# Two spare words ahead of the activations h and hh, and two behind them

## The reference, cut to what matters

```python
def modulate(x, g, shift, scale):
    return rms_norm(x, g) * (1.0 + scale[:, None, :]) + shift[:, None, :]

def swiglu(h, w_gate, w_up, w_down):
    return (jax.nn.silu(h @ w_gate) * (h @ w_up)) @ w_down

# first block, twice: x + 0.5 g * swiglu(h ...); x + g * mixer(h); x + 0.5 g * swiglu(h ...)
# second block, twice: proj = h @ w_in -> mixer -> x;  q = h2 @ peer_q, expert sums over h2 -> x
```

## The kernel before

| tensor | start | past a multiple of 64 |
|---|---|---|
| ring | 16512 | 0 |
| weights_hi | 32896 | 0 |
| arena | 49280 | 0 |
| more_lo | 80000 | 0 |
| x | 180352 | 0 |
| h (h_lo) | 188544 | 0 |
| hh (h_hi) | 196736 | 0 |
| vfirst | 204928 | 0 |
| work; work_1 (gat_lo) | 215072; 219168 | 32 |
| small (gat_hi) | 223264 | 32 |

## Time and profile before

### The profile page before, as it was taken

How to read it: one execution, slowest core, us unless ns; L and a number is a source line. 1 busy time by engine, 2 the same in 40 slices (tenths; PEclk the granted TensorE clock), 3 DMA queues, 4 the chain that set the end, 5 groups by cost and what they waited for, 6 DMA issues and landing times.

```text
span 3476.7 us, 68787 instructions
## 1 busy us (share of the span) xinstructions
PE 3342.0 (96%) x26804; PEld 3203.1 (92%) x26804; DVE 2579.5 (74%) x4576; ACT 1608.5 (46%) x2594; POOL 198.7 (6%) x331
## 2 busy tenths in 40 slices
PE   6999989999999998999999999999899999999998
PEld 5999869999967998889999999998789999999998
DVE  7889667888736896746977867776755977777776
ACT  3456644454445445134444444444414445444444
POOL 1100001101000220200000000000300000000000
PEclk9999999999999999999999999999999999999999
DMA  9964218979613993034664466665215665456665
GB/s 369 359 221 169 74 49 324 336 261 334 249 46 113 385 374 127 31 132 171 228 207 169 166 225 229 230 229 174 75 46 171 230 221 175 169 203 229 232 228 181
DMA packets 246578, 707.46 MB, mean 203 GB/s; under 512 B 27472, under 2 KB 93008, under 8 KB 244928
## 3 DMA queue, kind: packets, MB, share of 16 engines
q1 hardware_dynamic: 212112, 571.64, 47.2%
q0 software_dynamic: 34224, 132.46, 10.2%
HBM read 669.40 MB, written 34.60 MB: 202 GB/s over the span
## 4 chain that ended last, share of the span: by engine, by line
PE 85%; DVE 7%; DMA 4%; ACT 2%; issue 2%; SPq 0%; POOL 0%; DVEq 0%; ACTq 0%; POOLq 0%
PE psum L517 39%; PE psum L550 26%; PE psum L1074 3%; DMA ring<-stream 2%; PE psum L896 2%; PE psum L1009 1%; PE psum L647 1%; DVE ring L1641 1%; PE psum L916 1%; PE psum L498 1%; PE psum L529 1%; DMA arena<-mod_weights 1%; PE psum L530 1%; DVE arena L1569 1%; ACT weights_hi L1146 1%
## 5 line engine op out<-in xcount | busy, mean ns | idle before, releaser
L517 PE MATMUL psum<-hh,weights_hi 128*128 128x256 f32 x4216 | 1212.2, 288 | 19.2 <-ACT arena L1360 8.1
L1146 ACT ACTIVATE weights_hi<-ring 128x1024 fp32r<-128x1024 f32 x711 | 752.0, 1058 | 993.6 <-DMA ring<-stream 928.6
L517 PE MATMUL psum<-h,weights_hi 128*128 128x256 f32 x4216 | 1197.5, 284 | 0.0
L1641 DVE TENSOR_TENSOR ring<-ring,weights_hi 128x1024 fp32r<-128x1024 f32 x711 | 870.1, 1226 | 440.0 <-ACT weights_hi L1146 434.9
L517 PE MATMUL psum<-hh,ring 128*128 128x256 f32 x2976 | 845.5, 284 | 0.0
L517 PEld LDWEIGHTS psum<-hh,weights_hi 128*128 128x128 f32 x4216 | 814.2, 193 | 26.8 <-issue 11.3
L517 PEld LDWEIGHTS psum<-h,weights_hi 128*128 128x128 f32 x4216 | 814.1, 193 | 0.3
L550 PE MATMUL psum<-small,weights_hi 128*128 128x256 f32 x2752 | 774.5, 281 | 4.9 <-DVE work L1665 3.3
L550 PE MATMUL psum<-work,weights_hi 128*128 128x256 f32 x2752 | 772.1, 281 | 0.0
L550 PE MATMUL psum<-small,ring 128*128 128x256 f32 x2304 | 646.1, 280 | 0.0
L517 PEld LDWEIGHTS psum<-hh,ring 128*128 128x128 f32 x2976 | 574.9, 193 | 0.0
(11 more groups left out here) (410 smaller groups left out, 3897.0 us busy)
## 6 DMA issues: line engine op xcount, KB each, us to landing
ring<-stream SPq DMA_DIRECT2D x735, 512.0 KB, 3.6
arena<-mod_weights POOLq DMA_DIRECT2D x224, 512.0 KB, 6.3
arena<-stream SPq DMA_DIRECT2D x222, 512.0 KB, 5.7
acts<-small SPq DMA_DIRECT2D x256, 128.0 KB, 2.2
work<-acts SPq DMA_DIRECT2D x256, 128.0 KB, 2.2
arena<-cond_rows POOLq DMA_DIRECT2D x3, 1024.0 KB, 7.6
arena<-w_uq POOLq DMA_DIRECT2D x1, 3072.0 KB, 10.3
arena<-constants POOLq DMA_DIRECT2D x2, 1200.0 KB, 5.7
```

The costliest lines, as they stand in the source:

```text
L517: mm = pe.matmul(out, lhs[:, d, :], rhs[:, d, :], start=(d == 0 and p == 0), stop=(d == DT - 1 and p == 2))
L1146: act.activation(whi[:, NTH[n] % WS, :], raw(n), ACT.Copy).then_inc(sem["block_hi"], 1)
L1641: dve.tensor_tensor(low(n), raw(n), whi[:, NTH[n] % WS, :].bitcast(F32), ALU.subtract)\
```

## The change

Two tensors of two float32 words in a partition (8 bytes) that nothing reads or writes are allocated, `line_half` between x and h, and `line_rest` between hh and vfirst. No instruction is added, removed or moved; only addresses differ. h and hh move by what `line_half` takes, and all tensors behind hh by what both take.

```diff
         x = sb("x", [P, DT, T])
 
+        sb("line_half", [P, 2])
         h, (h_lo,) = sb_twice("h", [P, DT, T], [([P, DT, T], F32R)])
         hh, (h_hi,) = sb_twice("hh", [P, DT, T], [([P, DT, T], F32R)])
+        sb("line_rest", [P, 2])
         vfirst = sb("vfirst", [P, 4, T])
```

## The result

The changed kernel took 3451.73 us (median of 4 runs, 3450.79 to 3454.97), the kernel before 3478.12 us (4 runs, 3474.61 to 3479.54): a ratio of 0.9926, 95% interval 0.9912 to 0.9940, so 26 us or 0.74% less. The profiled execution of the changed kernel has a span of 3448.9 us, 27.8 us under that of before.

What follows compares the result with a forecast made beforehand. TensorE's matmul streams were taken as the bound, chiefly lines 517 and 550. 25.0 us of TensorE time x 0.88 on the path gave 22 us, other terms 0: 3476.7 - 22 = 3454.5 us, range 3440 to 3482.

Steps and rivals of the forecast that it cites:

- What bounds the kernel: TensorE works through 96% of the span; line 517 holds 38.5% of it on the chain, line 550 another 26.2%.
- The addresses: Each new tensor starts on a multiple of 32, so h at 188576 and hh at 196768, 32 past a multiple of 64.
- The cause: The moving operand's start by 64 sets the matmul rate: line 517 at 120.0 ns, line 550 at 117.4 to 118.7; chance 0.64.
- what is left is the place of the moving operand: Line 684 changes output like line 550 yet takes 120.0 ns, so operand place remains, reuse and writes not told apart.
- The size of a matmul's gain: Line 517: 2.6 ns less in feed-forwards, 1.35 in expert layers, 2.0 elsewhere; with lines 529, 530, 543, 25.0 us of TensorE time.
- front's 720: Matmuls of lines 529, 530 and 543, which read h and hh too: 720 x 2.0 ns, 1.4 us.
- The share on the path: The chain holds 1338 of line 517's 1518 us, 0.88, so 22 of 25.0 us reach the time.
- The prediction's last sentence: An effect of h's place relative to the weights' place, not the remainder by 64, would make the forecast wrong at once.
- the prediction's cover of the transfers: Transfers at 99% in the first feed-forward may bring weights late to a faster TensorE; 2.6 us at stake, kept for the range.
- The terms at nothing: Taken as 0: line 550's rate, DVE's and ACT's passes over h, the final store of h, line 647's mask reads.
- The passes over h and hh: DVE's and ACT's three passes at the head of a sublayer, 480, 478 and 495 ns: taken as 0, bound 0.9 us.
- The rule of column counts: Spacing by column counts alone, 109 ns a matmul and 107 ns a weight load, so the change is worth nothing.

Runs made afterwards that it cites:

- the first run: Sixteen spare words (64 bytes) ahead of h and sixteen behind hh in place of two, against the kernel before: 3458.9 us, 23 under it.

## Why the prediction was right, and where it wasn't

**What bounds the kernel: right.** The chain's long pieces of lines 517 and 550 were the place to read, and a gain of 3 ns for a matmul is what moved the time.

**The addresses: right.** The build gave 188576 and 196768, as the table of starts led one to expect; a true 8 bytes would have brought little (119.3 ns over all starts of the run with both at 8, against 119.9).

**The cause: the wrong step.** The step from "what is left is the place of the moving operand" to "the remainder by 64 sets the rate" failed. The runs with 64 bytes and with the weights moved show the distance from the weights in its place: 117.8 ns with h on a multiple of 64 at distance 64, and the changed kernel's 114.80 us with h on a multiple of 64 at distance 32. The rows of before could not tell the two apart: their moving operands had only distance 0 (h, hh, more_lo) and 160 (small, work), which are also remainders 0 and 32. The prediction's last sentence named the distance, but it gave it no chance and no price. That the forecast came true is partly luck: h went to distance 32, not to the 160 of line 550, and 32 happens to be a fast place too. For distance 96, which has the same remainder by 64, the same reasoning would have forecast the same gain, and `rows_in_parts` was at 120.0 ns there in two kernels.

**The size of a matmul's gain: too small.** I took line 550's 117.4 to 118.7 for line 517 and so 25.0 us of TensorE time. Line 519 reached 116.7 and 117.8 nearly everywhere; over all starts that follow within 135 ns the mean went from 119.9 to 117.0, which is 2.9 ns, or some 37 us over 12,648 matmuls, and some 2 us more in front's 720.

**The share on the path: too large.** I took 0.88. Of some 39 us estimated from the starts, 27.8 reached the span, 0.71; of the 33.6 us by which TensorE's busy time fell over all lines, 0.83. What lies between 39 and 33.6 is in part line 552, which gave some 2 us back (118.1 to 118.3 ns over 8,256 matmuls); its distance went from 160 to 224. The rest, some 3 us, is not taken apart. What lies between 33.6 and 27.8 is TensorE's idle time, which grew by 5.8 us. The waits of line 519 on the split of weight blocks (waited for: us in total, times, longest) were 3.8 us in all in the kernel before; after, and then in the kernel with all at 192:

```profile
PE psum L519 <- DVE ring L1643: 9.0, 8, 4.3
...
PE psum L519 <- DVE ring L1643: 10.4, 10, 4.8
```

The split comes right behind the load of a block, and the chain's share of the loads into ring rose from 2.1% to 3.6% after and to 5.8% at 192. So a faster TensorE does meet its weights more often, as the prediction's cover of the transfers said; it is not only in the first feed-forward, whose piece of 984 has no gap. The two errors, a gain for each matmul of 2.9 ns in place of 1.9 and a share of 0.71 to 0.83 in place of 0.88, go against each other, which is why 22 us forecast and 26 measured lie so near. (3476.7 less 22 is 3454.7; the forecast's 3454.5 is a slip of 0.2 us.)

**The terms at nothing: right but for line 550.** Its rate was forecast not to change because its remainder stayed, and it cost the 2 us named above: the same wrong step. The passes over h and hh have medians of 480, 480 and 495 ns, where they had 480, 478 and 495.

**The rule of column counts.** The prediction set a rule of column counts alone against the rows. In fourteen profiles the same shape went at rates from 113.3 to 121.0 ns with nothing changed but addresses, so the traces don't agree with it here. The prediction also read the section too narrowly: the Trainium skill (TensorE: Matmul & The Clock Gate, section "Back-to-back issue gap") gives the formula behind 109 ns for a matmul by itself, and for streams of weight load and matmul pairs it gives measured spacings of about 81 ns at 128 columns and 131 ns at 512. All rates here, at 256 columns, lie between these two.

## What to carry to other kernels

Where a stream of matmuls bounds the kernel, compare the rates of lines with equal shapes, from starts and not from durations; if they differ, list the addresses of both operands, and try the distance of the moving tile from the weight tile. Read more than one stretch, because one placement can show several rates. It costs a few spare words and here was worth 1.9% (0.9812, 0.9796 to 0.9828). A difference seen between two lines gives a place to look, but two places on a scale don't say what the scale is: move each operand by itself, and both together.

## What the runs showed of the hardware that was not expected

- The rate of a weight load and matmul pair (128x128 weights, 256 columns in fp32r) depends in these runs on the distance between the two operands in a partition, with a pattern that repeats every 256 bytes: 120.0 ns at 0 and at +256, 113.3 at best at 192. That both are read from the same memory at the same time suggests a meeting of the two reads there. This is argued, not shown: no run shows where they would meet or what repeats after 256 bytes.
- The Trainium skill (SBUF — State Buffer, section "Who interferes with whom") calls TensorE's two read ports independent and says that TensorE never waits on anyone. The runs here show a rate that depends on where the two operands lie to each other, so by the measurement the spacing of the pairs depends on the addresses of both reads together; that one port waits for the other is not shown.
- A stream settles into one of a few exact rates and keeps it for hundreds of matmuls. With all at 192 it holds 113.3 in one stretch and 117.8 in another, in the run with h alone at 32 the first and third feed-forwards hold 117.0 and the second and the expert layers 120.0, and in the first run line 552 holds 116.7 in one feed-forward and 120.0 in the next. What selects the rate stays open. Most of the changes from one to the other follow a gap in the stream or matmuls of another line, but with all at 192 a few come with neither (near 2669, 2689 and 3257 us); no run was made for it.
